# Attention scores as 64x64 quarter-array products, the next tile's first half behind a place of dense products, and late second halves in two other PSUM banks

## The reference

```
for bi in range(3):                       # (window, dilation) = (128,1), (512,4), (2048,16)
    q: (1024 tokens, 8 heads, 64);  k, v: (1024 tokens, 2 heads, 64), each shared by 4 query heads
    s = einsum('nqhgd,nqkhd->nqhgk', q_blk, kg) * 64**-0.5 + bias     # bias: -slope_h * distance
    s = where(valid, s, -inf)             # a query reads keys at distances 0, d, 2d, .., window
    p = softmax(s);  o = p @ v;  lse = log-denominator
out = sum over branches of softmax(lse)[branch] * o;  x = x + out @ w_o
```

## Time and profile before

| | |
|---|---|
| median of 3 runs | 2703.72 us (2703.11 to 2706.36) |
| the profiled execution | 2703.66 us, its span 2701.9 us |
| TensorE busy | 2628.7 us, 97% of the span |
| VectorE busy | 1521.0 us, 56% |
| ScalarE busy | 826.3 us, 31% |
| the attention loop | from about 1634 to 1928 us of the span |

### The profile page before, as it was taken

The page is one execution under the profiler, slowest core; times in us unless marked ns, Lnnn a source line. Parts: engine busy times, 40 slices in busy tenths (PEclk is TensorE's granted clock), DMA queues, the critical chain, the costliest instruction groups (busy, mean ns, idle before and its releaser), DMA issues.

```text
span 2701.9 us, 48320 instructions
## 1 busy us (share of the span) xinstructions
PE 2628.7 (97%) x20366; PEld 2497.8 (92%) x20366; DVE 1521.0 (56%) x3231; ACT 826.3 (31%) x1871; POOL 69.5 (3%) x92
## 2 busy tenths in 40 slices
PE   7999999997899999999999999999999999999998
PEld 6999999995699999999999998786899999999997
DVE  6777777777465444444444734556754444444445
ACT  5544444544132111211121413446521112111211
POOL 0000000000300000000000000003100000000000
PEclk9999999998999999999999999999999999999999
DMA  3111111134311111111111224326111111111111
GB/s 143 56 50 49 35 33 41 42 127 165 107 48 47 47 48 47 47 48 47 48 48 47 100 84 126 103 75 207 47 47 48 47 47 48 47 47 48 48 32 63
DMA packets 85451, 178.03 MB, mean 66 GB/s; under 512 B 21809, under 2 KB 49705, under 8 KB 84521
## 3 DMA queue, kind: packets, MB, share of 16 engines
q1 hardware_dynamic: 76233, 162.72, 18.7%
q10 hardware_dynamic: 9008, 12.26, 1.4%
HBM read 143.95 MB, written 36.24 MB: 67 GB/s over the span
## 4 chain that ended last, share of the span: by engine, by line
PE 85%; DVE 8%; ACT 3%; DMA 1%; issue 1%; POOL 0%; SPq 0%; ACTq 0%; DVEq 0%
PE psum L2142 19%; PE psum L2143 19%; PE psum L2144 19%; PE psum L2216 3%; PE psum L2217 3%; PE psum L2218 3%; PE psum L2671 2%; PE psum L2417 2%; PE psum L2168 2%; PE psum L2631 1%; PE psum L2694 1%; PE psum L2632 1%; PE psum L2633 1%; PE psum L2509 1%; DMA x_half<-in_x 1%
## 5 line engine op out<-in xcount | busy, mean ns | idle before, releaser
L2142 PE MATMUL psum<-x_hi,w_hi 128*128 128x352 f32 (+1 forms) x1040 | 334.8, 322 | 0.0
L2143 PE MATMUL psum<-x_lo,w_hi 128*128 128x352 f32 (+1 forms) x1040 | 332.4, 320 | 0.0
L2144 PE MATMUL psum<-x_hi,w_lo 128*128 128x352 f32 (+1 forms) x1040 | 330.8, 318 | 0.0
L1164 DVE SCALAR_TENSOR_TENSOR w_lo<-w_raw,gains,w_hi 128x512 fp32r<-128x512 f32 x380 | 262.1, 746 | 74.7 <-ACT w_hi L625 74.6
L625 ACT ACTIVATE w_hi<-w_raw,gains 128x512 fp32r<-128x512 f32 x380 | 246.9, 712 | 122.4 <-DMA w_raw<-in_w 122.1
L2216 PE MATMUL psum<-x_hi,w_hi 128*128 128x352 f32 (+1 forms) x768 | 272.8, 355 | 2.7 <-DVE pre L1246 2.7
L2142 PE MATMUL psum<-u_hi_b,w_hi 128*128 128x352 f32 (+1 forms) x768 | 247.1, 322 | 0.0
L2142 PE MATMUL psum<-u_hi,w_hi 128*128 128x352 f32 (+1 forms) x768 | 246.8, 321 | 0.0
L2142 PE MATMUL psum<-x_hi_b,w_hi 128*128 128x352 f32 (+1 forms) x768 | 246.6, 321 | 0.0
L2217 PE MATMUL psum<-x_lo,w_hi 128*128 128x352 f32 (+1 forms) x768 | 246.1, 320 | 0.0
L2218 PE MATMUL psum<-x_hi,w_lo 128*128 128x352 f32 (+1 forms) x768 | 245.7, 320 | 0.0
(11 more groups left out here) (380 smaller groups left out, 5504.5 us busy)
## 6 DMA issues: line engine op xcount, KB each, us to landing
w_raw<-in_w SPq DMA_DIRECT2D x190, 512.0 KB, 3.8
q_tile<-scratch_q SPq DMA_DIRECT2D x24, 256.0 KB, 3.0
scratch_att<-o_out ACTq DMA_DIRECT2D x32, 132.0 KB, 2.7
x<-in_x SPq DMA_DIRECT2D x8, 516.0 KB, 9.5
s_state<-in_s_rec_in SPq DMA_DIRECT2D x2, 2048.0 KB, 15.1
out_s_rec<-s_state SPq DMA_DIRECT2D x8, 512.0 KB, 2.6
merge<-scratch_att SPq DMA_DIRECT2D x8, 512.0 KB, 3.9
dec<-scratch_gates ACTq DMA_DIRECT2D x7, 512.0 KB, 3.4
```

What stands on the lines that cost most here:

```text
L1164: done = v.scalar_tensor_tensor(w_lo[:, slot, 2 * part + k], w_raw[:, part, k], gains[:, unit * UW + 2 * part + k:unit * UW + 2 * part + k ...
L2142: mm(out, whi, xh[:, k, cols], start=k == 0, stop=False)
L2143: mm(out, whi, xl[:, k, cols], start=False, stop=False)
L2144: done = mm(out, wlo, xh[:, k, cols], start=False, stop=k == kts - 1)
```

## The change

The score product is cut in four. `k_mask` becomes `k_feat`, each key once, with no zeros; the memory set free holds `merge`, which earlier lay over the other half of `k_mask`. For each j, four products of 64 rows by 64 columns are issued: key head g (rows 64g of the array) and query half h (columns 64h), with nk blocks of 128 keys as the moving operand. Head 0 goes to the first bank of a pair, head 1 to the second. Every half now uses the pair of banks 3 and 4, but for the second halves of tiles 19 to 21, which use banks 1 and 2.

TensorE signals once a half (`scores_full`), and before it writes a pair it waits until all four VectorE instructions of the pair's last use are done (`max_ready`). In steps 0 to 17 the scores of tile s+1.0 are issued behind the second fill of the step and not ahead of it. VectorE writes a key projection in one instruction of 128 partitions instead of two of 64, and no longer clears the zeros of `k_mask`.

```diff
+def score_pair(step, hs):
+    return (1, 2) if hs and 18 < step < 22 else (3, 4)
...
             def scores(nxt, hs):
                 b, tile, par, nk = nxt
                 if hs == 0:
                     pe.wait_ge(sem(f"part{par}_landed"), L.next(f"part{par}_landed", 16))
-                keys = k_mask[:, b % 2, :, (tile + 1 - nk) * P:(tile + 1) * P]
+                cols = slice((tile + 1 - nk) * P, (tile + 1) * P)
+                step = tiles.index(nxt)
+                pair = score_pair(step, hs)
+                if pair in used:
+                    pe.wait_ge(sem("max_ready"), 4 * (used[pair] + 1))
+                elif pair == (3, 4):
+                    for free in ("bank3_free", "bank4_free"):
+                        pe.wait_ge(sem(free), L.next(free)), L.skip(free, -1)
+                else:
+                    pe.wait_ge(sem("product_free"), taken["products"])
+                used[pair] = 2 * step + hs
                 for j in (2 * hs, 2 * hs + 1):
-                    bank = hs if nk == 1 else j % 2
-                    if nk == 2 or j % 2 == 0:
-                        pe.wait_ge(sem(f"bank{3 + bank}_free"), L.next(f"bank{3 + bank}_free"))
-                    lo = (j % 2) * 2 * P if nk == 1 else 0
-                    done = mm(psum[:, 3 + bank, lo:lo + 2 * nk * P].rearrange("p (g c) -> p g c", g=2), q_tile[:, par, j], keys,
-                              start=True, stop=True)
-                    if nk == 2 or j % 2:
-                        done.then_inc(sem(f"bank{3 + bank}_full"), L.add(f"bank{3 + bank}_full"))
+                    lo = j % 2 * nk * P
+                    for g in range(2):
+                        rows = slice(g * HD, (g + 1) * HD)
+                        for h in range(2):
+                            part = slice(h * HD, (h + 1) * HD)
+                            done = mm(psum[part, pair[g], lo:lo + nk * P], q_tile[rows, par, j, part], k_feat[rows, b % 2, cols],
+                                      start=True, stop=True, tile_position=(g * HD, h * HD))
+                done.then_inc(sem("scores_full"), L.add("scores_full"))
...
+                if step < 18:
+                    fill(3 * step + 1)
                 if step < 23:
                     scores(tile_of(step + 1), 0)
-                fill(3 * step + 1)
+                if step >= 18:
+                    fill(3 * step + 1)
...
             def biased(step, nxt, hs):
+                cols = slice((2 - nk) * P, 2 * P)
+                pair = score_pair(step, hs)
+                v.wait_ge(sem("scores_full"), L.next("scores_full"))
                 for n in range(4 * hs, 4 * hs + 4):
-                    m = n % 4
-                    bank = 3 + m // 2 if nk == 2 else 3 + hs
-                    per = 2 if nk == 2 else 4
-                    if m % per == 0:
-                        v.wait_ge(sem(f"bank{bank}_full"), L.next(f"bank{bank}_full"))
...
+                    lo = n % 4 // 2 * nk * P
+                    v.tensor_tensor_reduce(prob[:, par, n, cols], psum[:, pair[n % 2], lo:lo + nk * P], bias[:, n, cols],
+                                           -1.0, -NEG, ALU.add, ALU.min, stats[:, step % 3, 0, n:n + 1]
+                    ).then_inc(sem("max_ready"), L.add("max_ready"))
...
                 if tiles == 2 and tile == 0:
-                    for g in range(2):
-                        rows = slice(g * HD, (g + 1) * HD)
-                        done = v.tensor_tensor(by_class(k_mask[rows, b % 2, g]), src[rows], scale[rows], ALU.mult)
-                        done.then_inc(sem(mark if g else "dve_order"), L.add(mark if g else "dve_order"))
+                    v.tensor_tensor(by_class(k_feat[:, b % 2]), src, scale, ALU.mult).then_inc(sem(mark), L.add(mark))
...
                 if n == 0:
-                    for g in range(2):
-                        v.memset(k_mask[(1 - g) * HD:(2 - g) * HD, :, g], 0.0).then_inc(sem("dve_order"), L.add("dve_order"))
                     v.wait_ge(sem(L.last), L.value(L.last))
-                    v.sem_inc(sem("k_zeroed"), L.add("k_zeroed"))
+                    v.sem_inc(sem("k_begun"), L.add("k_begun"))
```

More of the change, by code:

```diff
@@ L312, in build @@
     a = area(region + KT * NT * 4)
-    k_mask = at("k_mask", [P, 2, 2, SEQ], F32, a)
+    k_feat = at("k_feat", [P, 2, SEQ], F32, a)
+    merge = at("merge", [P, 2, 2, 8 * HD], F32, a)
     v_feat = at("v_feat", [P, 2, SEQ], F32, a)
@@ L359, in build @@
     block = ctx.enter_context(nc.Block())
+    taken = {}
     halves = [slice(0, HALF), slice(HALF, SEQ)]
@@ L469, in store_keys @@
                 rows = slice(g * HD, (g + 1) * HD)
-                sp.dma_start(t["p_k"][rows, b], k_mask[rows, b % 2, g]
+                sp.dma_start(t["p_k"][rows, b], k_feat[rows, b % 2]
                 ).then_inc(sem("kv_stored"), L.add("kv_stored", 16))
@@ L505, in attention_traffic @@
                 weight(U_KVQ + 3, part)
-            sp.wait_ge(sem("k_zeroed"), L.next("k_zeroed"))
+            sp.wait_ge(sem("k_begun"), L.next("k_begun"))
             for dst, name in ((dist, "dist"), (slopes, "slopes")):
@@ L997, in exps @@
                 cols = slice((2 - nk) * P, 2 * P)
-                skip(*((3, 4) if nk == 2 else (3 + hs,)))
                 for n in range(4 * hs, 4 * hs + 4):
-                    bank = 3 + n % 4 // 2 if nk == 2 else 3 + hs
-                    if n % 2 if nk == 2 else n % 4 == 3:
-                        act.wait_ge(sem(f"bank{bank}_free"), L.value(f"bank{bank}_free"))
-                    else:
-                        act.wait_ge(sem("max_ready"), L.next("max_ready"))
+                    act.wait_ge(sem("max_ready"), L.next("max_ready"))
                     act.activation(prob[:, par, n, cols], prob[:, par, n, cols], ACT.Exp, scale=-1.0,
@@ L2047, in drain @@
                         kv_ready()
+                    if n == 29:
+                        taken["products"] = L.value("product_free")
                 for n in range(output_done(place - 2) // UW, output_done(place - 1) // UW):
@@ L2645, in output_step @@
                         pe.wait_ge(sem("raw_free"), L.next("raw_free", 4))
+                        pe.wait_ge(sem("max_ready"), 4 * (used[1, 2] + 1))
                     if n in (10, 15):
@@ L2659, in output_step @@
                     done.then_inc(sem("product_full"), L.add("product_full"))
+            tiles = [tile_of(i) for i in range(24)]
+            used = {}
             def scores(nxt, hs):
@@ L2790, in attention_layer @@
                 if m == 48:
-                    for free in ("bank5_free", "bank0_free", "bank3_free", "bank4_free"):
+                    for free in ("bank5_free", "bank0_free"):
                         pe.wait_ge(sem(free), L.next(free)), L.skip(free, -1)
+                    pe.wait_ge(sem("max_ready"), 4 * (used[3, 4] + 1))
                 output_step(m)
```

10 lines of the change are left out of this document (removed).

## The result

The changed kernel takes 2709.42 us (median of 20 runs, 2700.20 to 2717.82), and the kernel before, run beside it, 2704.26 (20 runs, 2700.13 to 2710.14). The ratio is 1.0017, with a 95% interval of 1.0009 to 1.0025: slower by 4.6 us (5.2 by the medians), where 2699.3 was forecast and the range ended at 2706. The profiled execution of the changed kernel took 2710.91 us, its span is 2709.1.

What follows compares the result with a forecast made beforehand. TensorE, busy 97% of the span, was taken to bound the kernel. From 2703.66 us, 12.2 us of shorter score blocks came off and 7.8 us of new waits were added: 2699.3 us, 8-in-10 range 2691 to 2706.

Steps and rivals of the forecast that it cites:

- rival D: Each of five new waits (steps 2 to 5 and 8) halves TensorE's clock: +7.5 us, 2706.8 us; chance 0.07.
- steps 2 to 5: Second halves' scores newly wait for VectorE's reads of the first: 1.24 us each, against 0.32 saved on first halves.
- step 8: Scores 8.1 wait 4.05 us for VectorE, a 1.86 us wait goes: net 2.1 us, against 0.73 saved.
- steps 19 to 21: Bound by a VectorE and GpSimd loop, so shorter scores gain nothing; if wrong, up to 3.6 us gained.
- steps 9 and 11: The wait ahead of second halves' scores was there in part already; no loss from it, 0.32 saved on first halves.
- step 18: The wait ahead of second-half scores was there in part already; no new wait, 0.73 us saved.
- Step 10: The new wait for VectorE adds 0.5 us, against 0.73 saved on the first half.
- Rival A: The new waits don't show, because VectorE reaches first halves earlier than now: 2691.5 us; chance 0.14.
- steps 12 to 17: Shorter score blocks save in full, with no new waits: 5.2 us.
- steps 22 and 23: Shorter score blocks save in full near the loop's end: 1.4 us.
- Rivals C and E: C: VectorE or ScalarE late in steps 12-17, 22-23, 2703 us, 0.11. E: tiles only two at a time, 2727 us, 0.08.
- The change of shape: Going from first halves' score tiles to the value product's tiles costs 0.10 us, within bounds 0 and 0.36.

Runs made afterwards that it cites:

- e6: Changed kernel plus 42 dense products nobody reads, in steps 8, 9 and 11 ahead of the second halves' scores; 2705.6 us.
- e11: Changed kernel with the first dense place ahead of second halves' scores in steps 1 to 17, and the first `merge` loads issued in step 16; 2691.5 us.
- e9: Changed kernel with second halves of tiles 19 to 21 in banks 3 and 4 like all others, without the one wait the other banks needed; 2709.3 us.
- e12: As e11, with the quarter-array rounds of the halves issued in steps 19 to 21 issued twice; 2689.5 us.
- e10: Changed kernel with the first two loads of `merge` and `merge_stats` issued in step 16, not at the end of step 17; 2705.1 us.
- e4: Changed kernel with first halves' scores back ahead of the step's second dense place, where they stood before; 2712.6 us.
- e5: Changed kernel with the first dense place ahead of the second halves' scores in steps 1 to 17; 2695.4 us, run again 2699.3 us.
- e8: Kernel before, with score products of the eight halves issued in steps 18 to 21 cut from 512 to 256 columns; 2706.3 us.

## Why the prediction was wrong

**The step that failed** is the clock. The sum has no term for it, and rival D got 0.07, on the ground that waits of 1.3 to 1.9 us had not brought it down before. The new ones in steps 2 to 5 didn't either (1.17 to 1.32 us, clock 1.00). But the 3.94 us of step 8 did, in every profile that has them, and so did the longer waits of steps 19 to 21; the 2.0 us of steps 9 and 11 did half of the time. In the profiled execution this is 5.5 us in steps 8, 9 and 11, and 0.9 + 1.05 in steps 19 and 21 (9.94 and 10.49 for 9.05 and 9.44). Another 19.62 - 15.91 = 3.7 us are in step 18, against e6; why the low clock lasts 11.8 us there stays open, as e6 has 3.4 us of it behind a wait of 2.60, and e11 has 6.8 with no wait in that step. With 1.6 (16.91 - 15.34) for a stretch of 3.4 us in step 1, which the profiles of e6 and e9 don't have with the same code there and which is not tied to the change, that is 12.7 us. Over all runs the clock went from 0.9913 to 0.9874, some 9 us by the slope of 2.25 (5 to 10 by the others). Rival D had the mechanism and came near the size, 7.5 us, but of its five places (steps 2 to 5 and 8) only step 8 was one, so the nearness is luck. The Trainium skill (TensorE: Matmul & The Clock Gate, A second HAM failure mode: psum-queue depth-cycling) tells of a kernel in which frequent short idling between groups of products made the clock go up and down. The windows of e6 (clock 1.00 for 0.88) and e12 (1.00 for 0.87) agree with it; the prediction didn't weigh that section.

**The waits.** Steps 2 to 5 were put at 1.24 - 0.32 = 0.92 us each; the intervals give 48.30 - 44.63 = 3.67, 0.92 each. Step 10 was put at 0.50 - 0.73 = -0.23 and has -0.23; steps 9 and 11 at -0.32, and have -0.31 with full clock (e6). Step 8 was put at 2.1 - 0.73 = +1.37 and has +0.36 with full clock (e6): too dear by 1.0. Half of that is an idle of 0.51 us ahead of scores 9.0 (at 1722.55 in the kernel before) that the prediction didn't see and that goes too; the rest stays open. Rival A is out.

**Step 18** was counted as no wait and 0.73 saved. It has +1.3 us at the same low clock (15.91 - 14.59). The prediction looked at the bank that became free, and not at the transfer ahead of VectorE's work on 18.0. Before, `merge_stats` was issued 2.9 us ahead of the value product of step 17 and used 1.6 us behind it; after, 1.0 us ahead (1841.29 for 1842.28) and 3.4 us behind. So TensorE now arrives early at a time that a transfer sets. e10 shows that the transfer is the cause; what holds its issue back was not followed.

**The savings.** In steps 12 to 17, where nothing waits, 5.2 us were forecast and 76.60 - 71.31 = 5.3 came, and in steps 22 and 23 1.4 and 1.6 us. A half with nk = 1 goes from 0.87 to 0.60 us start to start. Rivals C and E are out: the four tiles run side by side. The change of shape costs little (e4). That the steps together come to -3.5 us for a sum of -4.4 is in part luck: step 18 is 2.0 us worse than forecast and step 8 is 1.0 better.

**Steps 19 to 21** were put at nothing, and rightly, at full clock (9.06 and, in e9, 9.44). What was missed is that a gain that ends in idling isn't neutral here.

**The range** ended at 2706 though the text priced D at 2706.8 and had step 8 among its places. The clock needed a term of its own, and the range its bound: the 12.7 us above would have reached from 2699 to 2712 (they are known only from these runs).

## What to carry to other kernels

When a change takes work off TensorE, or adds a wait, list the new idling place by place, and cost the clock there as well as the wait: here it was about twice the net gain. Put work that is needed anyway into a wait that can't be avoided (e5, e11), or failing that useless work (e6, by a little; e12, in the clock and not clearly in the time). Read more than one profile before tying a low clock to a wait. And before counting a saving as full, look for a transfer further on that will now be waited for (e10).

## What the runs showed of the hardware that was not expected

- 42 added products of 352 columns whose result nobody reads made the kernel 3.9 us faster by the medians (e6; by the means 3.4, interval 0.5 to 6.3), and scores cut by half in eight halves made it no faster (e8, 2706.3 for 2705.6 of the kernel before beside it).
- Runs of one kernel differ by up to 17 us (2700.2 to 2717.8, changed kernel), and follow their mean clock (0.990 to 0.985) at about 2.25 us for 0.001. A single profile of such a kernel says little on the total, but steps 2 to 17 at full clock repeat to 0.05 us between profiles of the same code (after, e6, e9, e10).
- Products on 64x64 tiles with 128 and 256 moving columns run four at a time: sixteen records of 256 columns take 1.02 us from start to start (step 9 above), where the four whole-array records of 512 took 1.71. At that pitch the sixteen would take 3.42 one after another, 1.71 two at a time and 0.86 four at a time.
